# Sums of down's products added to the residual by transfers of GpSimd's queue, a third pair in down's first groups, and the older banks first behind w_out

## The reference

```
xn = rmsnorm(x, attn_norm);  proj = xn @ w_in
y_mla = latent attention(proj) @ w_mla_branch;  y_fox = forgetting attention(proj) @ w_fox_branch
h = x + (g_mla * y_mla + g_fox * y_fox) @ w_out
hn = rmsnorm(h, mlp_norm)
u = square(relu(hn @ w_up))            # 2048 -> 8192
h = h + u @ w_down                     # 8192 -> 2048
out = rmsnorm(h, final_norm)
```

## Time and profile before

| what | value |
|---|---|
| median of 3 runs | 1260.85 us |
| the profiled execution, its span | 1261.62 us, 1259.8 us |
| TensorE busy | 1248.0 us (99%), 5558 matmuls |
| VectorE busy | 991.2 us (79%) |
| ScalarE busy | 679.3 us (54%) |
| GpSimd busy | 138.1 us (11%) |
| mean granted TensorE clock | 0.999 |

### The profile page before, as it was taken

How to read it: one execution, slowest core, us unless ns; L and a number is a source line. 1 busy time by engine, 2 the same in 40 slices (tenths; PEclk the granted TensorE clock), 3 DMA queues, 4 the chain that set the end, 5 groups by cost and what they waited for, 6 DMA issues and landing times.

```text
span 1259.8 us, 14874 instructions
## 1 busy us (share of the span) xinstructions
PE 1248.0 (99%) x5558; PEld 1033.2 (82%) x5558; DVE 991.2 (79%) x1112; ACT 679.3 (54%) x825; POOL 138.1 (11%) x239
## 2 busy tenths in 40 slices
PE   9999999999999999999999999999999999999997
PEld 7888888888888888887888888888888878888876
DVE  6576566646766667577898998989998899989884
ACT  6645345544555444455656445655455655465653
POOL 0021101103221112010011000110001010000100
PEclk9999999999999999999999999999999999999999
DMA  9788857765887679678777657776657685578861
GB/s 333 254 285 280 262 164 221 223 198 183 286 257 213 215 279 293 210 237 263 270 253 236 206 201 236 243 242 204 236 188 246 220 266 188 194 234 252 276 217 67
DMA packets 83142, 293.90 MB, mean 233 GB/s; under 512 B 11320, under 2 KB 12416, under 8 KB 82432
## 3 DMA queue, kind: packets, MB, share of 16 engines
q1 hardware_dynamic: 67536, 243.04, 58.2%
q0 software_dynamic: 14528, 48.00, 12.6%
q10 hardware_dynamic: 1008, 1.92, 0.4%
HBM read 269.45 MB, written 23.47 MB: 233 GB/s over the span
## 4 chain that ended last, share of the span: by engine, by line
PE 79%; DVE 12%; DMA 4%; ACT 2%; issue 2%; POOL 0%; DVEq 0%; ACTq 0%; POOLq 0%
PE bank L739 44%; PE bank L785 11%; PE bank L787 11%; PE bank L786 11%; DVE hl L1322 5%; DMA turned<-turn_rows 2%; DMA turn_rows<-blocks 2%; DVE wsum_lo L1345 1%; ACT hl L1046 1%; DVE u_hl L1595 1%; ACT hid L1119 1%; DVE wsum L1332 1%; DVE blocks L1575 1%; PE bank L928 1%; PE bank L910 0%
## 5 line engine op out<-in xcount | busy, mean ns | idle before, releaser
L1322 DVE TENSOR_TENSOR hl<-raw,hl 128x1024 fp32r<-128x1024 f32 x327 | 397.1, 1232 | 186.5 <-ACT hl L1046 186.1
L1046 ACT ACTIVATE hl<-raw 128x1024 fp32r<-128x1024 f32 x327 | 340.6, 1055 | 279.2 <-PE bank L739 202.2
L739 PE MATMUL bank<-hl,x_hl 128*128 128x512 f32 (+1 forms) x1536 | 345.1, 386 | 0.0
L739 PEld LDWEIGHTS bank<-hl,x_hl 128*128 128x128 f32 x1536 | 284.6, 188 | 56.6 <-ACT hl L1037 0.5
L785 PE MATMUL bank<-hl,hn_hl 128*128 128x512 f32 x417 | 162.3, 389 | 1.4 <-DVE resid L1645 1.4
L787 PE MATMUL bank<-hl,hn_hl 128*128 128x512 f32 x417 | 162.2, 389 | 0.0
L786 PE MATMUL bank<-hl,hn_hl 128*128 128x512 f32 x417 | 162.2, 389 | 0.0
L1322 DVE TENSOR_TENSOR hl<-raw_more,hl 128x1024 fp32r<-128x1024 f32 x124 | 148.7, 1217 | 15.0 <-ACT hl L1046 14.4
L785 PE MATMUL bank<-hl,u_hl 128*128 128x512 f32 x363 | 142.0, 391 | 1.6 <-DVE u_hl L1595 1.5
L786 PE MATMUL bank<-hl,u_hl 128*128 128x512 f32 x363 | 141.4, 389 | 0.0
L787 PE MATMUL bank<-hl,u_hl 128*128 128x512 f32 x363 | 141.3, 389 | 0.0
(11 more groups left out here) (227 smaller groups left out, 1420.5 us busy)
## 6 DMA issues: line engine op xcount, KB each, us to landing
raw<-weights SPq DMA_DIRECT2D x330, 512.0 KB, 4.5
raw_more<-weights SPq DMA_DIRECT2D x124, 512.0 KB, 4.7
turn_rows<-blocks POOLq DMA_DIRECT2D x34, 512.0 KB, 3.8
turned<-turn_rows POOLq DMA_DIRECT2D x96, 128.0 KB, 5.0
prob_rows<-prob_blocks POOLq DMA_DIRECT2D x8, 384.0 KB, 2.8
prob_t<-prob_rows POOLq DMA_DIRECT2D x32, 96.0 KB, 5.7
turned_h<-turn_rows POOLq DMA_DIRECT2D x20, 128.0 KB, 4.9
x_rows<-x_n POOLq DMA_DIRECT2D x2, 1024.0 KB, 8.9
```

The costliest lines, as they stand in the source:

```text
L739: return nc.tensor.matmul(bank[:, gr.pair + tb, 0:gr.cols], tile[:, k, x_part, tb * P:tb * P + P], w, start=k == 0 and not x_part and not ...
L1046: nc.scalar.activation(hl[:, slot, 0], raw_unit(u), ACT.Copy).then_inc(unit_hi, 1)
L1322: nc.vector.tensor_tensor(hl[:, slot, 1], raw_unit(u), hl[:, slot, 0].bitcast(F32), ALU.subtract).then_inc(unit_split, 1)
```

## The change

1. `pairs_by_seven` gives all down groups the three pairs of `SEVEN`. The second groups had them; the first group of down0, down1, down2 and down3 gets the pair k2 anew.
2. `into_resid` is gone. Every double group sums its products in `hid` (`sum_products`), and for a down group two transfers of GpSimd's queue add `hid` to `resid` (512 KB each, `accum_op=add`) once its totals are in `resid` (`add_into_resid`). What reads or writes `resid` or `hid` next waits for them: ScalarE's copy of the next double group's first product, VectorE's totals of the next down group, and the final norm's work.
3. `totals` of an up group is three instructions in place of four: the two left banks in one of 1024 columns.
4. In the table of due units: the second "hidden turns" from `last + 7` to `last + 6`; "u turned" from `last + 9 + 4c` to `last + 10 + 4c`; "u summed" from `last + 10 + 4c` to `last + 11 + 4c`; the squares of the last down's left columns from `last + 3` and `last + 6` to `last + 8` and `last + 9`, their gains from `last + 6`, `last + 7` to `last + 9`, `last + 11`.
5. Behind `w_out` the first group of up0 takes its first two units into the pair of banks that was left first, where it took the left pair first.

```diff
-    return SEVEN if (... and g == 0) or (name[:4] == "down" and g == 1) else FEWER
+    return SEVEN if (... and g == 0) or name[:4] == "down" else FEWER
...
-            steps = (14, 15) if gr.name[:2] == "up" else (14, 15, 16, 20)
-            for step, later in enumerate(steps):
-                due[gr.u0 + later].append(("products summed", (gr, step)))
+            for step in range(2):
+                due[gr.u0 + 14 + step].append(("products summed", (gr, step)))
...
-                due[gr.last + 3 + 4 * c].append(("hidden turns", piece))
-                due[gr.last + 9 + 4 * c].append(("u turned", piece))
+                due[gr.last + 3 + 3 * c].append(("hidden turns", piece))
+                due[gr.last + 10 + 4 * c].append(("u turned", piece))
...
-                    due[gr.last + 10 + 4 * c].append(("u summed", piece))
+                    due[gr.last + 11 + 4 * c].append(("u summed", piece))
...
+            def add_into_resid(gr):
+                pool.wait_ge(totals_done, gr.freed[-1])
+                for c in range(2):
+                    pool.dma_start(resid[:, :, chunk(2 * gr.g + c)], hid[:, 1 + 2 * c:3 + 2 * c],
+                                   accum_op=ALU.add).then_inc(resid_whole, 16)
...
-                    for c in range(2):
+                    older_first = sorted(range(2), key=lambda c: (gr.before, gr.before_right)[c].last)
+                    for c in older_first:
...
+                    else:
+                        act.wait_ge(resid_whole, 32 * (had.m + 1))
```

More of the change, by code:

```diff
@@ L85, in pairs_by_seven @@
 def pairs_by_seven(name, g):
-    return SEVEN if (name[:2] == "up" and name != "up0" and g == 0) or (name[:4] == "down" and g == 1) else FEWER
+    return SEVEN if (name[:2] == "up" and name != "up0" and g == 0) or name[:4] == "down" else FEWER
 LAST_DOWN = f"down{MLP_PARTS - 1}"
@@ L176, in number_groups @@
                 gr.m, n_up = n_up, n_up + 1
-                gr.freed = [n_totals + i for i in (1, 2, 3, 4)]
             else:
                 gr.m, n_down = n_down, n_down + 1
-                gr.freed = [n_totals + i for i in (1, 1, 2, 3)]
+            gr.freed = [n_totals + i for i in (1, 1, 2, 3)]
             n_totals = gr.freed[-1]
@@ L250, in make_due @@
             for c in range(2):
-                due[gr.last + 3 + 3 * c].append(("chunk squared", Chunk(gr.name, 2 * gr.g + c)))
-                due[gr.last + 6 + c].append(("chunk gained", Chunk(gr.name, 2 * gr.g + c)))
+                due[gr.last + 8 + c].append(("chunk squared", Chunk(gr.name, 2 * gr.g + c)))
+                due[gr.last + 9 + 2 * c].append(("chunk gained", Chunk(gr.name, 2 * gr.g + c)))
         if gr.name[:2] == "up":
@@ L715, in _ @@
                 take_turn(key, turned[:, n % 2])
+                if key[0][:2] == "up" and key[1] == FF_CHUNKS - 1:
+                    for gr in DOUBLES:
+                        if gr.name == "down" + key[0][2:]:
+                            add_into_resid(gr)
         @block.tensor
@@ L1141, in square_chunk @@
             def square_chunk(gr, norm):
-                if gr.name == LAST_DOWN and gr.g == 0:
-                    act.wait_ge(totals_done, BY[LAST_DOWN, 0].freed[1])
-                elif gr.name == LAST_DOWN and gr.g == 1:
-                    act.wait_ge(resid_whole, DOWN_DOUBLES)
+                if gr.name == LAST_DOWN and gr.g < CHUNKS // 2:
+                    act.wait_ge(resid_whole, 32 * DOWN_DOUBLES)
                 else:
@@ L1380, in into_resid @@
-            def into_resid(gr, step):
-                left, right = chunk(2 * gr.g), chunk(2 * gr.g + 1)
-                if step == 0:
-                    dve.wait_ge(p1_copied, gr.n + 1)
-                    dve.wait_ge(totals_done, gr.freed[0] - 1)
-                    nc.vector.tensor_tensor(resid[:, 0, left], resid[:, 0, left], bank[:, 4], ALU.add)
-                    then_wait(nc.vector.tensor_tensor(hid[:, 0], bank[:, 6], hid[:, 1], ALU.subtract))
-                elif step == 1:
-                    then_wait(nc.vector.tensor_tensor(hid[:, 2], hid[:, 0], bank[:, 7], ALU.add))
-                    then_wait(nc.vector.tensor_tensor(resid[:, 1, left], resid[:, 1, left], hid[:, 2], ALU.subtract))
-                elif step == 2:
-                    nc.vector.tensor_tensor(hid[:, 3:5], hid[:, 0:3:2],
-                                            bank[:, 5].unsqueeze(1).broadcast_to([P, 2, WIDE]),
-                                            ALU.add).then_inc(products_summed, 1)
-                else:
-                    dve.wait_ge(products_summed, gr.n + 1)
-                    dve.wait_ge(totals_done, gr.freed[-1])
-                    nc.vector.tensor_tensor(resid[:, :, right], resid[:, :, right], hid[:, 3:5],
-                                            ALU.add).then_inc(resid_whole, 1)
@@ L1412, in totals_into_resid @@
                 nc.vector.tensor_tensor(resid[:, 1, right], resid[:, 1, right], bank[:, 3], ALU.add).then_inc(totals_done, 1)
-            def gain_chunk(g):
-                c = chunk(g)
-                dve.wait_ge(gain_rows_in, 16)
-                if g == 0:
-                    dve.wait_ge(totals_done, BY[LAST_DOWN, 0].freed[1])
-                else:
-                    dve.wait_ge(resid_whole, DOWN_DOUBLES)
-                nc.vector.tensor_tensor(final[:, :, c], resid[:, :, c],
-                                        gain_rows[:, c].unsqueeze(1).broadcast_to([P, TB, WIDE]),
-                                        ALU.mult).then_inc(gained, 1)
             def totals(gr):
                 dve.wait_ge(products_summed, gr.n + 1)
-                dve.wait_ge(block_left, 3 * gr.n + 1)
-                nc.vector.tensor_tensor(hid[:, 1], bank[:, 0], hid[:, 1], ALU.add).then_inc(totals_done, 1)
                 dve.wait_ge(block_left, 3 * gr.n + 2)
-                nc.vector.tensor_tensor(hid[:, 2], bank[:, 1], hid[:, 2], ALU.subtract).then_inc(totals_done, 1)
+                nc.vector.tensor_tensor(hid[:, 1:3], bank[:, 0:2], hid[:, 1:3], ALU.add).then_inc(totals_done, 1)
                 dve.wait_ge(block_left, 3 * gr.n + 3)
@@ L1436, in totals, with gain_chunk @@
                 nc.vector.tensor_tensor(hid[:, 4], bank[:, 3], hid[:, 4], ALU.add).then_inc(totals_done, 1)
+            def gain_chunk(g):
+                c = chunk(g)
+                dve.wait_ge(gain_rows_in, 16)
+                dve.wait_ge(resid_whole, 32 * DOWN_DOUBLES)
+                nc.vector.tensor_tensor(final[:, :, c], resid[:, :, c],
+                                        gain_rows[:, c].unsqueeze(1).broadcast_to([P, TB, WIDE]),
+                                        ALU.mult).then_inc(gained, 1)
             def turn_hidden(piece):
@@ L1716, in _ @@
                     elif what == "products summed":
-                        gr, step = g
-                        if gr.name[:2] == "up":
-                            sum_products(gr, step)
-                        else:
-                            into_resid(gr, step)
+                        sum_products(*g)
                     elif what == "chunk gained":
```

15 lines of the change are left out of this document (7 added, 8 removed).

## The result

The changed kernel takes 1276.12 us, the median of four runs (1274.64 to 1277.38); the kernel before, timed beside it, 1260.88 (1260.19 to 1261.51). The ratio is 1.0115, with a 95% interval from 1.0101 to 1.0130: slower by 15.2 us, where 10.5 had been forecast, inside the range given. The profiled execution took 1274.64 us, span 1272.8.

What follows compares the result with a forecast made beforehand. VectorE's queue ahead of k8 in down's first groups was taken as the bound, not TensorE. 11.9 us for four groups less 1.4 at the seam gave 1260.85 + 10.5 = 1271.3 us, range 1266 to 1278.

Steps and rivals of the forecast that it cites:

- What bounds the kernel: Down's first groups: TensorE, 99% busy, waits for VectorE before k8; rival that TensorE is the bound: 1256.7 us, chance 0.05.
- Sums for k2, k3's wait: Down's first groups, at k3: VectorE does k2's weight sums first, so TensorE loses 0.95 us.
- The second transposition, k6's wait: Down's first groups, at k6: with the transposition moved ahead of k6, TensorE gets the first rest 0.46 us later.
- "u turned", k8: Down's first groups, at k8: `u_hl` ends at 24.22, TensorE starts at 24.38 instead of 21.81; 2.57 us lost, largest term.
- "u summed", k10: Down's first groups, pair k10: the row sums' rest comes behind k10's sums and unit; TensorE waits 0.75 us.
- The groups' total: Four first groups of down: k12 starts at 35.33 against a mean of 32.24; 2.98 us per group, 11.9 us together.
- Removed adds and transfers: Down groups: removing VectorE's adds gains 0 and the adding transfers keep nobody; 0 to 0.5 us in all.
- Older banks: Seam of `w_out` and up0: TensorE's 1.41 us wait goes, -1.4 us; at worst it returns at k10 or k12, 0.5 to 1.4.
- The clock: Rival, k8 and k9 of down's first groups: half speed, 4 x 4.7 = 19 us, 1290; over 1278 by this or late rows: 0.07.

Runs made afterwards that it cites:

- the narrow sums: Changed kernel with pair k2's sums in down's first groups 32 columns wide instead of 512, on VectorE and ScalarE; 1268.86 us, ratio 1.0057.

## Why the prediction was right, and where its sizes were off

**What bounds the kernel.** Right: TensorE is 98% busy and is not what these groups wait for. 12 matmuls fewer and 15.2 us more is the plainest evidence; the two kernels, one without the third pair and one with nothing else, show that both parts lengthen VectorE's queue, and the narrow sums show that it is the time of the sums that costs, since matmuls, waits and order stayed as they were.

**Sums for k2, k3's wait.** Forecast 0.95; measured 0.90, 0.87, 0.88 and 0.88 beyond the pitch of two matmuls, and 0.10 to 0.11 more at the next start. The trace follows the chained queue: unit k2 was forecast at 5.25 and stands at 5.38 (665.25 - 659.87), the transposition at 6.39 and 6.52, k3 at 8.40 and 8.52. The 0.13 was there from the last total on.

**The second transposition, k6's wait.** Forecast 0.46, measured 0.79 in down0 and 0.37 to 0.43 in the others. Most of the difference in down0 is the 0.30 us for the copy of the first transposition, which the text had called on the edge and priced at nothing.

**"u turned", k8.** Forecast 2.57, start at 24.38; measured 2.36 to 2.40, starts at 24.77, 24.40, 24.38 and 24.46. The rows were back in time, as argued. The Trainium skill ("Perfetto Trace Analysis", Identifying the Most-Contended Engine) would have one optimize the engine with the highest occupancy first; no occupancy changed by more than a point here, and the order of waits told what the occupancy could not.

**"u summed", k10.** Forecast 0.75, measured 0.65 to 0.69; in down2 the slow matmuls hide it.

**The groups' total.** From its first matmul to the start of the next group, the first group lasts 46.75, 46.45 and 47.24 us in down0 to down2, where it lasted 42.65, 43.65 and 43.42; to its last matmul it lasts 46.20 in down3, where it lasted 43.13. That is 13.8 us more, against 11.9 forecast. k12, forecast at 35.33, starts at 35.87, 35.57, 36.35 and 35.54. Of the 1.9 missing, 0.8 is the clock's fall in down2 (1.5 less the hidden wait at k10) and 0.3 is the copy in down0. The rest is 0.2 in every part: pair k10 starts at 30.69 in down1 and down3 where 30.57 was forecast, and the second matmul behind its wait 0.08 late.

**Removed adds and transfers.** Priced at 0 to 0.5; the run with the transfers alone gives 0.4 to 2.6 us. TensorE and VectorE never wait for them, as argued, and ScalarE does once, 1.0 us off the path, where the text had said that they keep nobody. The bound was probably too narrow, and what the loss comes from stays open.

**Older banks.** Forecast -1.4 us, with the wait at worst coming back at k10 or k12 of up0, so that 0.5 stays. The worse end is nearer to what came. The seam's wait did go (573.83 starts without one), but 0.33 + 0.77 came back in up0, where VectorE waited 2.33 us for weights (1.14 at that place before); the run with this part alone gives a gain of 0.8 with an interval down to none. That the later loads are what brings the waits back is read from the traces and not tested. The stretch from up0's start to down0's start, 84.44 us before, is 86.04 after; down0 starts 0.85 us earlier than before (659.87 against 660.72), not 1.4.

**The clock.** The prediction kept full speed in its sum and a chance of 0.07 for a fall. It fell at one of the four places in the profiled execution, at two in the second one, at three with the narrow sums (all behind waits of 2.07 to 2.24 us), and at none with the third pair alone (waits of 1.57 to 2.12). It is a small term: about eight matmuls 0.2 us late, 1.5 us less what it hides behind it, not the 4.7 per group of that rival. The Trainium skill ("TensorE: Matmul & The Clock Gate", Part 1) says that the clock falls behind a stretch without work. The traces agree in kind: at half speed in six places behind waits of 2.07 to 2.24 us, at full speed in eight others behind waits just as long.

**The account of 15.2 against 10.5.** 1.9 in the groups and 0.6 at the seam, on top of the 10.5, make the profiled execution 13.0 above that of before. The other 2.2 lie in the medians: the profiled execution of before was 0.74 above its median of 1260.88, that of after 1.5 below. The second series of the changed kernel lies 12.6 us above its own runs of before (1274.73 against 1262.09), so these 2.2 us may be chance.

**Not settled:** why the clock falls behind one 2.2 us wait and not behind the next, and what the 0.4 to 2.6 us of the transfers are. In neither of the two tables is there room for the third pair without these waits: VectorE's own work up to `u_hl` ends 22.4 us behind the first matmul with the older table (23.62 less 1.20 of rests) and 23.7 with the new one (24.72 less 1.06), and TensorE is at k8 after 20.4. No run made the sums of k2 earlier, ahead of the totals of the up group, as those of k6 and k10 are made ahead; that is untested.

## What to carry to other kernels

Read an engine's room in the stretch where the new work goes, and behind which wait it ends, not in its share of the span: VectorE, at 79%, was full just there, and pairs done with an eighth less of TensorE's work made the kernel slower. When work is due "one unit later", list everything that stands between the two places in that engine's queue; a unit that brings sums of its own is five times as much (5.6 us against 1.14). A wait taken away at a seam can come back behind the next loads: of 1.4 us, 0.85 were left in the profiled execution when down0 began.

## What the hardware showed unexpectedly

- Behind waits of 2.1 to 2.2 us TensorE's clock fell to half in some places and not in others, up to 1.6 us after the first matmul that followed; behind 7.4 and 7.8 us it fell every time (five waits), and in down0 of the kernel with "u turned" one unit later still it was at half before the waiting matmul started.
- An adding transfer of 512 KB from one buffer on the chip to another took 1.18 to 1.73 us to issue and 6.4 us (median) to land, against 0.56 and 3.8 to 4.0 for a plain one of that size to memory.
- Turned rows for which ScalarE waited needed 14.0 us from transposition to first read in down0 of the kernel before, and with the second transposition behind k8's split 10.0 us in down0 and 17.0 us in down3. What sets the way's length no run shows.
